# Fillings put between the two heads' transposes, rope taken sooner, and another order of query tiles in the last pair of heads

## The chip, the cores and the metric

One core of a Trainium2 chip runs the whole kernel. The metric is the device time of one execution in microseconds, lower being better.

## The reference

A decoder trunk of two layers over 1024 positions of width 1024, in float32. The change lies in layer 0, whose mixer feeds two head groups from one projection: eight heads A (dilated sliding-window softmax attention, head width 64, partial rotary) and four heads B (gated linear attention, GLA). Shortened:

```python
z = h @ w_in
qa, ka, va, qb, kb, vb, rb, gl = jnp.split(z, offs, axis=-1)
qa = partial_rope(split_heads(qa, N_HEADS_A), positions)
ka = partial_rope(split_heads(ka, N_HEADS_A), positions)
oa = dilated_attention(qa, ka, split_heads(va, N_HEADS_A))      # causal softmax, three dilations
ob = gla(split_heads(qb, N_HEADS_B), split_heads(kb, N_HEADS_B), split_heads(vb, N_HEADS_B), ...)
ob = rms_norm(ob, g_out_b) * jax.nn.silu(split_heads(rb, N_HEADS_B))
o = jnp.concatenate([merge_heads(oa), merge_heads(ob)], axis=-1)
return o @ w_out
```

A gated feed-forward layer follows, then layer 1 with its own feed-forward, and a last norm.

## The kernel before

Every float32 matrix product is made of three products of high and low parts (`hi*hi`, `lo*hi`, `hi*lo`). The eight heads A are worked in four pairs of heads (`hp` 0 to 3), the queries in tiles of 128 (`qt` 0 to 7). The loop of the attention goes over 32 *pairs* `n` of (pair of heads, query tile), in the order of `TILE_ORDER`. Since attention is causal, tile `qt` has `qt + 1` key tiles; they are handled in groups of four, so tiles 0 to 3 have one group (`groups(n) == 1`) and tiles 4 to 7 two. A *step* is one group of one pair. The queues of the engines are written out by hand, and each engine runs its queue in order.

TensorE (L1087 scores, L1100 transposes, L1108 and L1120 reciprocals and products with V) does at the first step of pair `n`: the *score block* of pair `n + 1` for both heads; a filling; the transposes of the first head's exponentials; the products of the step before; the transposes of the second head. Both heads' transposes use the same PSUM bank, so each waits until ScalarE has copied the one before (`take`, L2216). A *filling* is a number of pieces of the projections of the next pair of heads: 48 pieces of three 512-column matmuls each (L1019 to L1021) and two blocks of four transposes of V (T0 and T1, L1028), numbered 0 to 49. They end the parts V0 V1 T0 T1 K0 Q0 K1 Q1 with numbers 7, 15, 16, 17, 25, 33, 41 and 49, where 0 and 1 are the first and second half of the positions. `PIECES` says how many go into each filling. In the last pair of heads the fillings are pieces of the output projection instead (`wo_piece`, L1062 to L1064, by `WO_PIECES`). They need the split outputs of the heads, which ScalarE (`split_high`, L2220) and VectorE (`split_low`, L1694) make in the order of `WO_HIGHS` and `WO_LOWS`.

VectorE takes the row maximum of each head's score block (`top(U)`, L1660, `U = 2n + h`; the next score block waits for the maxima of the last pair), the reciprocals of the sums (`recip`, L1667 and L1671), the output (`take_out`, L1678 and L1680) and the projected parts: V by `take_v` (L1619), K and Q by `rope` in three stages (shuffle and two multiplications; sum and high part; low part: L1635 to L1648). In the first three pairs it also finishes the GLA heads (`out_step`, L1558 to L1571, 128x1024 each). ScalarE makes the exponentials (`exp`, L2205) and copies T0 and T1 (`take_vn`, L2196). GpSimd splits each weight in a high part (L594) and a low part (L597), once the projection that used the buffer has ended. Query tiles 4 to 7 need the rope of K1 and Q1:

```python
pe.wait_ge(A.rope, 20 * hp + (10 if qt < 4 else 20))
if n:
    pe.wait_ge(A.max, 2 * n)
```

## Time and profile before

| | |
|---|---|
| Time, median of 3 runs | 2145.39 us (2144.12 to 2146.19) |
| The profiled execution: its time, its span | 2148.89 us, 2147.1 us |
| TensorE busy | 2103.5 us (98%) |
| VectorE, ScalarE, GpSimd busy | 1486.9 us (69%), 877.8 us (41%), 882.1 us (41%) |
| Granted TensorE clock, mean | 0.996 |
| The attention's loop | from about 243 to 507 us of the span |

Busy time is the time in which an engine had an instruction running. Because TensorE is busy nearly throughout, time shows as lost where its rows carry an idle time in brackets, with what released it, or where a matmul takes longer than its like. Times in the timeline count from the start of the span.

### The profile page before, as it was taken

The page shows a single profiled execution, that of the slowest core. Times are in us where ns is not written, and L with a number is a line of the kernel's source. Part 1 is how long each engine was busy: PE and PEld are TensorE (multiplying, and loading weights), DVE is VectorE, ACT ScalarE, POOL GpSimd, SP SyncE. Part 2 cuts the span into 40 slices and gives each one's busy share as a digit, 9 for nine tenths or more (in the row PEclk, how much of TensorE's full clock was granted, in tenths as well). Part 3 has the DMA queues.
Part 4 walks back from the last instruction along what each step waited for, and adds up shares of the span by engine and source line. Part 5 has one row for each costly group of instructions (what it writes and reads, how often), then busy time and mean ns, then how long its engine had stood idle before and what let it go on. Part 6 is the DMA issues. An engine that isn't in the chain of part 4 may idle for free.

```text
span 2147.1 us, 26169 instructions
## 1 busy us (share of the span) xinstructions
PE 2103.5 (98%) x10190; PEld 1710.9 (80%) x10190; DVE 1486.9 (69%) x1663; ACT 877.8 (41%) x1122; POOL 882.1 (41%) x459
## 2 busy tenths in 40 slices
PE   8999899999999999999999999999999999999997
PEld 5878677767788888888888888888788888888886
DVE  6659865573796767767798803337967767686987
ACT  4231234352554444445344431025544444444444
POOL 4323211122387776772000333433776777730000
PEclk9999999999999999999999999999999999999999
DMA  4111000003322222214986111113222222239872
GB/s 167 40 30 40 30 21 21 21 21 118 118 82 86 89 89 85 82 70 159 389 297 252 59 40 40 43 46 128 79 88 79 81 76 89 89 107 378 311 282 79
DMA packets 95100, 236.10 MB, mean 110 GB/s; under 512 B 10082, under 2 KB 12419, under 8 KB 94979
## 3 DMA queue, kind: packets, MB, share of 16 engines
q1 hardware_dynamic: 93106, 229.70, 30.0%
q10 hardware_dynamic: 1872, 4.74, 0.6%
q8 instruction: 81, 1.33, 0.3%
q14 instruction: 41, 0.33, 0.0%
HBM read 198.75 MB, written 35.65 MB: 109 GB/s over the span
## 4 chain that ended last, share of the span: by engine, by line
PE 85%; DVE 9%; ACT 2%; issue 2%; DMA 2%; SPq 0%; DVEq 0%; ACTq 0%
PE ps L1214 12%; PE ps L1216 11%; PE ps L1215 11%; PE ps L1248 6%; PE ps L1250 6%; PE ps L1251 6%; PE ps L809 5%; PE ps L812 5%; PE ps L815 5%; PE ps L1019 2%; PE ps L1021 2%; PE ps L1020 2%; DMA d_ring<-g_kept 2%; PE ps L1100 1%; PE ps L1120 1%
## 5 line engine op out<-in xcount | busy, mean ns | idle before, releaser
L594 POOL TENSOR_TENSOR w_hi<-w_raw,ones 128x1024 fp32r<-128x1024 f32 x56 | 112.6, 2011 | 776.4 <-PE ps L815 235.6
L1214 PE MATMUL ps<-t_hi,w_hi 128*128 128x512 f32 x672 | 263.9, 393 | 1.9 <-ACT snap L2323 1.5
L1216 PE MATMUL ps<-t_hi,w_lo 128*128 128x512 f32 x672 | 261.7, 389 | 0.0
L1215 PE MATMUL ps<-t_lo,w_hi 128*128 128x512 f32 x672 | 261.6, 389 | 0.0
L1248 PE MATMUL ps<-d_hi 128*128 128x512 f32 (+1 forms) x640 | 244.7, 382 | 0.9 <-DVE d_lo L1910 0.7
L1251 PE MATMUL ps<-d_hi,d_lo 128*128 128x512 f32 (+1 forms) x640 | 243.9, 381 | 0.0
L1250 PE MATMUL ps<-d_lo,d_hi 128*128 128x512 f32 (+1 forms) x640 | 243.9, 381 | 0.0
L640 POOL TENSOR_TENSOR w_lo<-w_sum,w_hi 128x1024 fp32r<-128x1024 f32 x84 | 232.7, 2780 | 23.9 <-ACT w_hi L2326 23.9
L640 POOL TENSOR_TENSOR w_lo<-w_raw,w_hi 128x1024 fp32r<-128x1024 f32 x84 | 158.4, 1885 | 175.3 <-ACT w_hi L2326 157.5
L1214 PE MATMUL ps<-act_hi,w_hi 128*128 128x512 f32 x504 | 196.2, 389 | 0.7 <-POOL w_lo L640 0.7
L1215 PE MATMUL ps<-act_lo,w_hi 128*128 128x512 f32 x504 | 196.1, 389 | 0.0
L1216 PE MATMUL ps<-act_hi,w_lo 128*128 128x512 f32 x504 | 196.1, 389 | 0.0
L809 PE MATMUL ps<-act_hi,w_hi 128*128 128x512 f32 x592 | 185.2, 394 | 2.7 <-DVE act_lo L1408 1.3
L812 PE MATMUL ps<-act_lo,w_hi 128*128 128x512 f32 x592 | 182.5, 389 | 0.0
L815 PE MATMUL ps<-act_hi,w_lo 128*128 128x512 f32 x592 | 182.3, 389 | 0.0
L1214 PEld LDWEIGHTS ps<-t_hi,w_hi 128*128 128x128 f32 x672 | 126.1, 188 | 36.1 <-ACT snap L2323 10.3
L597 POOL TENSOR_TENSOR w_lo<-w_raw,w_hi 128x1024 fp32r<-128x1024 f32 x56 | 149.7, 2673 | 4.4
L2326 ACT ACTIVATE w_hi<-w_sum 128x1024 fp32r<-128x1024 f32 x84 | 89.1, 1061 | 151.5 <-PE ps L1216 111.0
L2310 ACT ACTIVATE ps<-fz,cw 128x1024 f32<-128x1024 f32 x88 | 105.6, 1202 | 108.1 <-DVE fz L1875 100.9
L1216 PEld LDWEIGHTS ps<-t_hi,w_lo 128*128 128x128 f32 x672 | 126.1, 188 | 26.5
L1215 PEld LDWEIGHTS ps<-t_lo,w_hi 128*128 128x128 f32 x672 | 126.2, 188 | 25.6
L1867 DVE TENSOR_TENSOR fz<-ps,snap 128x512 f32<-128x512 f32 x40 | 27.7, 692 | 167.2 <-PE ps L1216 167.2
(307 smaller groups left out, 4530.7 us busy)
## 6 DMA issues: line engine op xcount, KB each, us to landing
w_raw<-w_up SPq DMA_DIRECT2D x44, 1024.0 KB, 4.9
d_ring<-w_dn SPq DMA_DIRECT2D x146, 256.0 KB, 7.8
d_ring<-g_kept SPq DMA_DIRECT2D x124, 256.0 KB, 9.3
g_kept<-gst SPq DMA_DIRECT2D x44, 512.0 KB, 2.6
w_raw<-w_in SPq DMA_DIRECT2D x24, 512.0 KB, 3.6
chain_a<-g_kept SPq DMA_DIRECT2D x44, 256.0 KB, 8.9
x_kept<-x SPq DMA_DIRECT2D x16, 512.0 KB, 8.6
x<-x_kept SPq DMA_DIRECT2D x16, 512.0 KB, 10.2
```

What stands on the lines that cost most here:

```text
L594: pool.tensor_tensor(w_hi[:, slot, :], w_raw[:, parity, :], ones[:, 0:1].to_broadcast([P, 1024]), ALU.mult).then_inc(s_whi, 1)
L597: pool.tensor_tensor(w_lo[:, slot, :], w_raw[:, parity, :], w_hi[:, slot, :].bitcast(F32), ALU.subtract).then_inc(s_wsplit, 1)
L640: pool.tensor_tensor(w_lo[:, slot, cols].rearrange("p (a j c) -> p a j c", j=4, c=P), src, w_hi[:, slot, cols].bitcast(F32).rearrange("p ( ...
L809: pe.matmul(out[:, cols], wh, act_hi_k[:, cols], start=first, stop=False)
L812: pe.matmul(out[:, cols], wh, act_lo_k[:, cols], start=False, stop=False)
L815: ins = pe.matmul(out[:, cols], wl, act_hi_k[:, cols], start=False, stop=last)
L1214: pe.matmul(out, wh, bh, start=(fresh and j == 0), stop=False, skip_group_check=True)
L1215: pe.matmul(out, wh, bl, start=False, stop=False, skip_group_check=True)
L1216: ins = pe.matmul(out, wl, bh, start=False, stop=(j == 3), skip_group_check=True)
L1248: pe.matmul(out, w[:, 0, wcols], w[:, 1, cols], start=(s == 0 and i not in (D6, D7)), stop=False, skip_group_check=True)
L1250: pe.matmul(out, w[:, 0, wcols], g[:, 1, cols], start=False, stop=False, skip_group_check=True)
L1251: return pe.matmul(out, g[:, 0, wcols], w[:, 1, cols], start=False, stop=(s == NBLK - 1), skip_group_check=True)
```

## The change

TensorE's filling moves from ahead of a step's transposes to between them, and at pairs of two groups the second filling follows the first step's second transposes. ScalarE makes the next pair's exponentials ahead of the second head's copy. VectorE's order changes: the output of the pair before comes ahead of the reciprocals, the first two stages of a part's rope are taken together as soon as its pieces have ended, and some GLA steps come behind the parts. In the last pair of heads the order of query tiles changes from 1 2 3 0 4 5 6 7 to 3 2 7 6 5 4 1 0; the projections now end in its first pair (pair 24) instead of its second, and the pieces of the output projection and the splits of its operand are dealt out anew.

```diff
-        TILE_ORDER = (tuple(range(ST)),) * (NHP - 1) + ((1, 2, 3, 0, 4, 5, 6, 7),)
+        TILE_ORDER = (tuple(range(ST)),) * (NHP - 1) + ((3, 2, 7, 6, 5, 4, 1, 0),)
...
         PIECES = ((10,), (7,), (9,), (6,), (3, 3), (2, 2), (2, 2), (2, 2))
-        PIECES = (PIECES,) * 2 + (((8,), (8,), (7,), (5,), (2, 2), (2, 2), (2, 2), (2, 2)),
-                                  ((4,), (2,), (), (), (), (), (), ()))
+        PIECES = (PIECES,) * 2 + (((10,), (7,), (9,), (5,), (3, 2), (2, 2), (2, 1), (2, 1)),
+                                  ((4,), (), (), (), (), (), (), ()))
-        WO_HIGHS = ((), (0,), (1, 2), (3, 4), (5, 6), (), (), ())
+        WO_HIGHS = ((0,), (1, 2), (3, 4), (5,), (6,), (), (), ())
...
-                fill(n, gi)
                 transposes(n, gi, 0)
                 if step:
                     values(*steps[step - 1])
+                if gi == 0:
+                    fill(n, 0)
                 transposes(n, gi, 1)
+                if gi == 0 and groups(n) == 2:
+                    fill(n, 1)
...
+            B_STEPS = (((1, 0), (1, 1), (1, 2)), ((0, 0), (0, 1)), ((0, 3), (0, 4)))
+            B_LATE_STEPS = (((1, 3), (1, 4)), ((0, 2),), ())
             for n in range(PAIRS):
                 first_parts, second_parts = parts_of(n, 0), parts_of(n, 1) if groups(n) == 2 else []
                 if n + 1 < PAIRS:
                     top(2 * n + 2)
                     if groups(n) == 1:
                         top(2 * n + 3)
+                if n:
+                    take_out(n - 1)
                 recip(n)
                 if n < 3:
-                    for h, step_n in (((1, 0), (1, 1), (1, 2), (1, 3), (1, 4)), ((0, 0), (0, 1), (0, 2)), ((0, 3), (0, 4)))[n]:
+                    for h, step_n in B_STEPS[n]:
                         out_step(1, h, step_n)
-                if n == 0:
-                    take_part(0, Q1, (1,))
-                if n:
+                if n and n != ST * (NHP - 1) + 1:
                     for target, part in parts_of(n - 1, groups(n - 1) - 1):
                         take_part(target, part, (2,))
                 for target, part in first_parts:
                     take_part(target, part, (0,))
+                    take_part(target, part, (1,))
+                    if n == ST * (NHP - 1):
+                        take_part(target, part, (2,))
                 if n == 0:
-                    take_part(0, Q1, (2,))
-                if n:
-                    take_out(n - 1)
-                if groups(n) == 2 and n + 1 < PAIRS:
-                    top(2 * n + 3)
-                for target, part in first_parts:
-                    take_part(target, part, (1,))
-                for target, part in second_parts:
-                    take_part(target, part, (0,))
-                    take_part(target, part, (1,))
+                    take_part(0, Q1, (1, 2))
                 if groups(n) == 2:
+                    if n + 1 < PAIRS:
+                        top(2 * n + 3)
                     for target, part in first_parts:
                         take_part(target, part, (2,))
+                    for target, part in second_parts:
+                        take_part(target, part, (0,))
+                        take_part(target, part, (1,))
+                if n < 3:
+                    for h, step_n in B_LATE_STEPS[n]:
+                        out_step(1, h, step_n)
...
             for n in range(PAIRS):
+                take(n, 0, 0)
+                if n + 1 < PAIRS:
+                    exp(2 * n + 2)
+                    if groups(n) == 1:
+                        exp(2 * n + 3)
                 for gi in range(groups(n)):
                     for target, part in parts_of(n, gi):
                         if part == T0 or part == T1:
                             take_vn(target, part - T0)
-                    for h in range(2):
-                        take(n, gi, h)
-                    if gi == 0 and n + 1 < PAIRS:
-                        exp(2 * n + 2)
-                if n + 1 < PAIRS:
-                    exp(2 * n + 3)
+                take(n, 0, 1)
+                if groups(n) == 2:
+                    take(n, 1, 0)
+                    take(n, 1, 1)
+                    if n + 1 < PAIRS:
+                        exp(2 * n + 3)
```

TensorE's queue at pair 5 (first pair of heads, query tile 5), from behind the score block of pair 6; `a_s` are the exponentials and `a_pt` their copied transposes. Before:

```order
L1019 MATMUL ps<-act_hi,w_hi 128x512
L1020 MATMUL ps<-act_lo,w_hi 128x512
L1021 MATMUL ps<-act_hi,w_lo 128x512
L1019 MATMUL ps<-act_hi,w_hi 128x512
L1020 MATMUL ps<-act_lo,w_hi 128x512
L1021 MATMUL ps<-act_hi,w_lo 128x512
L1100 MATMUL ps<-cst,a_s 128x128 x4
L1120 MATMUL ps<-a_pt,a_vn_131 64x128 x2
L1100 MATMUL ps<-cst,a_s 128x128 x4
```

The same place in the changed kernel:

```order
L1100 MATMUL ps<-cst,a_s 128x128 x4
L1120 MATMUL ps<-a_pt,a_vn_131 64x128 x2
L1019 MATMUL ps<-act_hi,w_hi 128x512
L1020 MATMUL ps<-act_lo,w_hi 128x512
L1021 MATMUL ps<-act_hi,w_lo 128x512
L1019 MATMUL ps<-act_hi,w_hi 128x512
L1020 MATMUL ps<-act_lo,w_hi 128x512
L1021 MATMUL ps<-act_hi,w_lo 128x512
L1100 MATMUL ps<-cst,a_s 128x128 x4
```

The two pieces moved from ahead of the first head's four transposes to between these and the second head's.

VectorE's queue where the rope of K1 for the last pair of heads stands, which is pair 23 before (query tile 7) and pair 22 in the changed kernel (tile 6); L1660 and L1663 are row maxima, `a_sh` the rope's scratch. Before:

```order
L1635 STREAM_SHUFFLE a_sh_143<-ps 128x512
L1636 TENSOR_TENSOR a_sh_143<-ps,ropeC 128x512
L1638 TENSOR_TENSOR a_sh_143<-a_sh_143,ropeS 128x512
L1678 COPY a_r<-ps 128x128
L1680 TENSOR_TENSOR oT<-ps,a_r 128x128
L1660 ISA a_s,tiny<-ps,lmul 128x256
L1660 ISA tiny 128x1
L1643 TENSOR_TENSOR a_sh_143<-a_sh_143 128x512
L1645 CAST a_kh_134<-a_sh_143 128x512
L1648 TENSOR_TENSOR a_kl_137<-a_sh_143,a_kh_134 128x512
```

In the changed kernel, whose lines on VectorE are numbered 3 higher:

```order
L1638 STREAM_SHUFFLE a_sh_143<-ps 128x512
L1639 TENSOR_TENSOR a_sh_143<-ps,ropeC 128x512
L1641 TENSOR_TENSOR a_sh_143<-a_sh_143,ropeS 128x512
L1646 TENSOR_TENSOR a_sh_143<-a_sh_143 128x512
L1648 CAST a_kh_134<-a_sh_143 128x512
L1663 ISA a_s,tiny<-ps,lmul 128x1024
L1663 ISA tiny 128x1
L1651 TENSOR_TENSOR a_kl_137<-a_sh_143,a_kh_134 128x512
```

The row maximum of the second head, now of 1024 keys, moved behind the rope's sum and high part.

TensorE's queue from just behind the last piece of Q1 to the first score block of the last pair of heads that needs all keys (512 columns, then more). Before, this is from pair 25 on:

```order
L1100 MATMUL ps<-cst,a_s 128x128 x3
L1108 MATMUL ps<-cst,a_rows 128x128
L1120 MATMUL ps<-a_pt,a_vn_132 64x128 x4
L1100 MATMUL ps<-cst,a_s 128x128 x3
L1087 MATMUL ps<-a_kh_134,a_qh_136 128x128 x2
L1087 MATMUL ps<-a_kl_137,a_qh_136 128x128 x2
L1087 MATMUL ps<-a_kh_134,a_ql_141 128x128 x2
L1100 MATMUL ps<-cst,a_s 128x128 x4
L1108 MATMUL ps<-cst,a_rows 128x128
L1120 MATMUL ps<-a_pt,a_vn_132 64x128 x6
L1100 MATMUL ps<-cst,a_s 128x128 x4
L1087 MATMUL ps<-a_kh_134,a_qh_136 128x512 x2
```

In the changed kernel, with the last piece itself as its first three rows:

```order
L1019 MATMUL ps<-act_hi,w_hi 128x512
L1020 MATMUL ps<-act_lo,w_hi 128x512
L1021 MATMUL ps<-act_hi,w_lo 128x512
L1100 MATMUL ps<-cst,a_s 128x128 x4
L1087 MATMUL ps<-a_kh_134,a_qh_136 128x512 x2
L1087 MATMUL ps<-a_kl_137,a_qh_136 128x512 x2
L1087 MATMUL ps<-a_kh_134,a_ql_141 128x512 x2
```

Of what stood between the last piece and that score block, four transposes are left.

## Rows read from the trace of the kernel before

**Rows 1.** Busy time in stretches: one per pair of heads, then around 266.

```profile
core 0: us, PE busy (x) PEld busy (x) DVE busy (x) ACT busy (x) POOL busy (x), PEclk, DMA share, GB/s
242.80:315.80 73.00, 65.48 (x432) 50.58 (x432) 53.77 (x105) 24.53 (x59) 15.33 (x8) 0.95 0.08 26
315.80:381.40 65.60, 64.08 (x449) 49.58 (x448) 38.52 (x95) 24.84 (x58) 13.20 (x7) 1.00 0.08 25
381.40:442.50 61.10, 60.16 (x433) 46.22 (x432) 36.94 (x89) 24.92 (x58) 11.60 (x5) 1.00 0.06 19
442.50:506.70 64.20, 57.99 (x421) 43.31 (x421) 36.75 (x81) 31.20 (x63) 15.52 (x7) 1.00 0.25 89
...
262.60:269.40 6.80, 4.68 (x13) 3.89 (x14) 6.46 (x13) 0.60 (x1) 0.00 (x0) 0.52 0.25 77
```

**Rows 2.** What TensorE waited for: us in total, times, longest.

```profile
PE ps L1028 <- DVE a_vt L1619: 5.5, 1, 5.5
PE ps L1100 <- ACT a_pt L2216: 5.5, 15, 0.8
```

**Rows 3.** Timeline of TensorE: start, us, engine, line, [idle before, releaser].

```profile
264.72 1.12 PE L1028 MATMUL ps<-cst,a_vt 128*128 128x128 f32 x4 [5.53 <-DVE a_vt L1619]
```

**Rows 4.** Timeline of VectorE ahead of the end of that wait.

```profile
256.61 2.92 DVE L1558 SCALAR_TENSOR_TENSOR b_st<-b_st,b_kd 128x1024 f32<-128x1024 f32 x1
259.56 3.25 DVE L1562 TENSOR_TENSOR b_st<-b_st,b_kd 128x1024 f32<-128x1024 f32 x1
...
263.98 0.68 DVE L1619 TENSOR_TENSOR a_vt<-ps,rstd 128x512 f32<-128x512 f32 x1
```

**Rows 5.** Timeline of GpSimd at the same place and near 437.

```profile
256.48 1.96 POOL L594 TENSOR_TENSOR w_hi<-w_raw,ones 128x1024 fp32r<-128x1024 f32 x1 [9.66 <-PE ps L1021]
258.52 3.20 POOL L597 TENSOR_TENSOR w_lo<-w_raw,w_hi 128x1024 fp32r<-128x1024 f32 x1
...
437.33 1.89 POOL L594 TENSOR_TENSOR w_hi<-w_raw,ones 128x1024 fp32r<-128x1024 f32 x1 [37.37 <-PE ps L1021]
439.31 2.71 POOL L597 TENSOR_TENSOR w_lo<-w_raw,w_hi 128x1024 fp32r<-128x1024 f32 x1
```

**Rows 6.** Timeline of TensorE: transposes at pairs 0 and 5.

```profile
250.35 0.27 PE L1100 MATMUL ps<-cst,a_s 128*128 128x128 f32 x1
251.07 0.30 PE L1100 MATMUL ps<-cst,a_s 128*128 128x128 f32 x1 [0.46 <-ACT a_pt L2216]
...
294.21 0.60 PE L1100 MATMUL ps<-cst,a_s 128*128 128x128 f32 x4
...
295.58 0.63 PE L1100 MATMUL ps<-cst,a_s 128*128 128x128 f32 x4 [0.41 <-ACT a_pt L2216]
...
297.43 0.38 PE L1100 MATMUL ps<-cst,a_s 128*128 128x128 f32 x2
```

**Rows 7.** Timeline of ScalarE at pair 6.

```profile
305.04 1.15 ACT L2205 ACTIVATE a_s<-a_s,tiny 128x1024 f32<-128x1024 f32 x1
...
306.19 0.47 ACT L2216 ACTIVATE a_pt<-ps 128x384 f32<-128x384 f32 x1
```

**Rows 8.** Timeline of VectorE: the rope of K1 beside GpSimd.

```profile
437.23 0.74 DVE L1635 STREAM_SHUFFLE a_sh<-ps 128x512 f32<-128x512 f32 x1
...
438.45 1.32 DVE L1638 TENSOR_TENSOR a_sh<-a_sh,ropeS 128x512 f32<-128x512 f32 x1
...
440.56 2.00 DVE L1643 TENSOR_TENSOR a_sh<-a_sh 128x512 f32<-128x512 f32 x1
442.59 0.43 DVE L1645 CAST a_kh<-a_sh 128x512 fp32r<-128x512 f32 x1
```

**Rows 9.** Timeline of VectorE: first and last rows of an undisturbed rope.

```profile
211.56 0.73 DVE L1635 STREAM_SHUFFLE a_sh<-ps 128x512 f32<-128x512 f32 x1
...
214.85 0.69 DVE L1648 TENSOR_TENSOR a_kl<-a_sh,a_kh 128x512 fp32r<-128x512 f32 x1
```

**Rows 10.** Timeline of TensorE: pair 24's score block, the closing matmuls.

```profile
442.50 0.44 PE L1087 MATMUL ps<-a_kh,a_qh 64*128 64x384 f32 x2
...
495.67 0.50 PE L1062 MATMUL ps<-act_hi,w_hi 128*128 128x512 f32 x1
```

More of the change, by code:

```diff
@@ L770, in build @@
         PIECES = ((10,), (7,), (9,), (6,), (3, 3), (2, 2), (2, 2), (2, 2))
-        PIECES = (PIECES,) * 2 + (((8,), (8,), (7,), (5,), (2, 2), (2, 2), (2, 2), (2, 2)),
-                                  ((4,), (2,), (), (), (), (), (), ()))
-        WO_HIGHS = ((), (0,), (1, 2), (3, 4), (5, 6), (), (), ())
-        WO_LOWS = ((), (), (0, 1), (2, 3), (4, 5), (6,), (), ())
-        WO_PIECES = ((0,), (0,), (0,), (4,), (2, 2), (2, 1), (1, 1), (1, 0))
+        PIECES = (PIECES,) * 2 + (((10,), (7,), (9,), (5,), (3, 2), (2, 2), (2, 1), (2, 1)),
+                                  ((4,), (), (), (), (), (), (), ()))
+        WO_HIGHS = ((0,), (1, 2), (3, 4), (5,), (6,), (), (), ())
+        WO_LOWS = ((), (0, 1), (2, 3), (4,), (5,), (6,), (), ())
+        WO_PIECES = ((0,), (0,), (2, 2), (2, 2), (1, 1), (1, 1), (2,), (0,))
         def fill_of(n, gi):
```

## The prediction

> **What bounds the kernel.** I read the share of busy time first: TensorE is busy 98% of the span, so only its idle time and its slow clock can be won back. The table by stretches says where those are inside the attention [rows 1]: 7.5 us idle in the first pair of heads, 1.5 and 0.9 us in the second and third, 6.2 us in the last (length less busy time of each of the first four rows). The list of who waited for whom names the first: one wait of 5.5 us for `a_vt`, and 15 short ones for `a_pt`, 5.5 us together [rows 2]. It ends at 264.72 [rows 3]. From 262.6 to 269.4 the granted clock was at 0.52, the lower of its two levels (1.2 GHz), with 4.68 us of TensorE's work in it (the fifth of [rows 1]): half of that, 2.3 us, is what the slow clock costs on top.
>
> Why the wait was so long is in VectorE's queue: two operations on two SBUF tensors, 1.2 us each when alone, take 2.92 and 3.25 [rows 4], while GpSimd splits a weight [rows 5]. They alternate: GpSimd's first split ends at 258.44 and VectorE's operation 1.1 us behind it; the second split, 2.4 us when alone, takes 3.20, and VectorE's next one ends 1.1 us behind that.
>
> **The change, part by part.** Times are relative to the trace of before; every instruction stays, so only waits and the overlap count.
>
> *Filling between the transposes (small waits).* At a step with one key group the second head's transposes start 0.72 us after the first's, where alone they need 0.11; with four key tiles 1.37 where work allows 0.96 [rows 6]. With a filling between, this is gone: -0.6 at pair 0, -0.36 at pairs 1 and 9, -0.4 at pairs 5, 13 and 21. In return a pair's first transposes now follow the last pair's second ones with only one score block between. The same 1.37 us holds there; where that block is short (the head changes at pairs 8 and 16, the pairs before them) it gives 1.14 and 0.96: +0.2 each, four times.
>
> *The 5.5 us wait.* TensorE stood there from 259.2 (264.72 less 5.53). It now comes 1.0 us sooner by pairs 0 and 1, but has pair 2's first transposes and pair 1's products (1.2 us) ahead: about 259.5. VectorE takes V's second half behind two GLA steps instead of three, but those two wait for GpSimd as before. Its queue by its own durations: the reciprocals' copy is held to 258.7, then a split of 2.4 us and two steps of 1.2 us: 263.4, against 263.98 [rows 4]. So the transposes start at 264.15, 0.6 sooner, and 1.2 us of work is already done: with pair 0's 0.6, which lies inside that wait and isn't added again, -1.75 in all. The wait is still about 4.6 us, and I take the clock to fall as before.
>
> *ACT's new order.* `exp` of the next pair's first head now stands ahead of this pair's second copy of the transposes, `take`. At pair 6 that `exp` starts at 305.04, because its row maxima stand behind K1's rope steps, and the next copy only at 306.19 [rows 7]. Count from the second group's transposes of pair 5, 297.43 [rows 6]: this copy then starts at +8.8 and pair 6's second group can be transposed at +9.5; by its own work TensorE is there at +7.9, so 1.6 us are lost. Before, 0.2 and 0.7 were lost there and some slack used: the stretch to the next score block was 10.92 us and becomes 11.54, +0.6 at pairs 6 and 14. Sum so far, first two pairs of heads: -1.75 - 0.4 + 0.6 + 0.4 = -1.15 and -0.36 - 0.4 + 0.6 + 0.4 = +0.25.
>
> *Third pair of heads.* Its pieces now end K1 at pair 22's first filling and Q0's first half at pair 20's. All of that rope's first two stages stand ahead of the second row maximum, on which the next score block waits. Pair 20: rope ends 3.1 us behind the filling, the maximum 0.95 later, TensorE is ready at 3.45: +0.85. Pair 22: K1's end also sets GpSimd going. The row shows what that does: from the shuffle at 437.23 the steps that take 0.68 alone took 1.32 and 2.00, and the cast began 5.36 us behind the shuffle [rows 8]. In before a score maximum and an output stood between and nobody waited. Now the maximum of 1024 keys (1.15 us) comes behind the cast: it ends 7.1 us behind the filling, while TensorE, after four transposes (0.4), a piece (0.8), three transposes (0.3), the products (1.2) and three transposes (0.5), is ready at 3.2: a wait of +3.9. Won: -0.1, -0.5 (pairs 17, 18: the two blocks of V transposes are apart), -0.4, -0.25. Sum: +0.85 + 3.9 - 1.25 = +3.5.
>
> The Trainium skill ("SBUF — State Buffer", section "SBUF: two separate sides") calls the port that VectorE and GpSimd share an exclusive lock, held by whichever started first for the whole instruction; the trace agrees, 2.00 us against 0.68. If they only slowed each other a little, the wait at pair 22 would be 1.3 us by the undisturbed rows.
>
> *Last pair of heads.* Query tile 7 comes third. Its scores need all of K and Q, and Q's last piece ends only in the filling just ahead. A rope that nothing disturbs takes 3.98 us from shuffle to the last low part [rows 9]; with 0.2 to start, TensorE, which has four transposes (0.59), waits 3.5 us at that score block. From there I went along the queues with the durations of before: waits of 0.5 and 0.4 us for the 1024-key maxima and exponentials, 0.4 at tile 6, 0.6 at tiles 5 and 4, 0.5 at the last two; then the 48 closing matmuls start 50.1 us behind the first score block, and two pieces (1.36 us) less are in it than in the 53.17 us of before [rows 10]. 51.46 against 53.17: -1.7. Its bounds: each `act_lo` operand or `take` one queue place later costs about 1 us, so -4 to +3.
>
> *The clock.* Before fell to half behind 5.5 us of idling. Two new waits idle TensorE 3.7 and 3.3 us. No row shows a wait between 2 and 5 us and what the clock did. Bounds: nothing, or the 2.3 us above each. They are nearer to the known wait than to none: I take 1.8 and 1.2 (the second partly hides under the next wait for VectorE).
>
> Sum: -1.15 + 0.25 + 3.5 - 1.7 = +0.9; with the clock +3.0: **+3.9 us**. It is made against the profiled execution (span 2147.1 us, 2148.9 with what lies around it), which is 3.5 above the median of the three runs; the difference carries over: 2145.4 + 3.9 = **2149.3 us**. 0.2% is 4.3 us, about what a measurement of this kernel can tell from no change, so this is within it, near its edge.
>
> **Rivals.**
> *A, the sum above*, 2149.3, own range 2145 to 2153.5 (a microsecond or so in each of the four stretches): 0.48.
> *B, the clock stays up at the new waits.* They are shorter than the one that is known to drop it. 2146.3; if it also stays up at the first, now 4.6 us: 2144.0. 0.2.
> *C, slower: in the last pair of heads copies queue behind exponentials.* Four large tiles follow each other; VectorE has `split_low` (1.2 us) and ScalarE `split_high` (1 us) ahead of each first maximum and copy. My walk gives 0.4 per tile because the short fillings just cover it. Once a first maximum ends over a microsecond later than I have it, each of the four pays pair 6's 1.6 us: 4 x 1.2 more, 2154.1. For it: [rows 7]. Against: the walk has slack at two of them. 0.2.
> *D, faster: VectorE gets ahead of GpSimd.* If its operations ask for the port first where the new order shifts them by tenths, the first wait shrinks to 0.9 us (-3.7) and the clock stays up (-2.3), pair 22 waits 1.3 instead of 3.9 (-2.6) with no fall (-1.8), and pairs 6 and 14 don't wait (-3.2): 2135.7. Against it: in every case of [rows 4, 8] VectorE was the one held. 0.12.
>
> **How the numbers follow.** Beyond 2149.7 lies somewhat under half of A and nearly all of C: slower 0.38. Faster (below 2141.1): most of D, and an error of mine in A or B: 0.18. Within: 0.44. The range, 2139 to 2155.5, holds A, B, most of C and a third of D.
>
> **What would show it.** In the profile after: a wait of 4 to 5 us at the transposes of V's second half, near 260; one near 3.9 us at the score block behind pair 22, released by a row maximum; one near 3.5 us at the first score block of 1024 keys of the last heads, released by `a_ql`; the waits of the first transposes for `a_pt` below 0.3 us, with 1.6 us at pairs 6 and 14. Wrong would make me: neither new wait over 2 us; a score block that another row releases; the last pair of heads shorter than 48 us or longer than 53 from its first score block of 384 keys to the 48 closing matmuls.

## The result, and the profile after

The changed kernel takes 2150.8 us (median of 9 runs, 2150.05 to 2155.05), the kernel before beside it 2145.6 us (9 runs, 2144.12 to 2148.29). The ratio is 1.0023, with a 95% interval from 1.0014 to 1.0031. That is 4.9 us slower by the ratio and 5.2 by the two medians, where +3.9 was forecast; 2150.8 stands against a forecast of 2149.3.

The profiled execution took 2151.1 us. Its page, the span and the first row of busy time:

```profile
span 2149.3 us, 26169 instructions
...
PE 2106.8 (98%) x10190; PEld 1713.0 (80%) x10190; DVE 1490.2 (69%) x1663; ACT 879.0 (41%) x1122; POOL 883.9 (41%) x459
```

The share is 98% as before, so the page says nothing more. The stretches say where the time went. This is the answer to the same question as [rows 1], cut at the score blocks that are issued in pairs 0, 8, 16 and 24 and at the closing matmuls; the last three lines are the stretches at half clock:

```profile
core 0: us, PE busy (x) PEld busy (x) DVE busy (x) ACT busy (x) POOL busy (x), PEclk, DMA share, GB/s
240.25:311.96 71.71, 65.94 (x432) 50.78 (x432) 53.16 (x105) 24.71 (x59) 15.36 (x8) 0.95 0.09 26
311.96:377.84 65.88, 64.10 (x449) 49.51 (x448) 38.89 (x95) 25.03 (x58) 13.15 (x7) 1.00 0.08 25
377.84:446.38 68.54, 63.50 (x439) 48.34 (x438) 38.59 (x91) 25.77 (x58) 11.52 (x5) 0.98 0.08 24
446.38:498.93 52.55, 47.71 (x367) 34.91 (x366) 31.65 (x74) 29.95 (x62) 12.00 (x6) 0.94 0.06 19
260.37:267.20 6.83, 6.08 (x17) 4.93 (x18) 6.25 (x13) 2.00 (x5) 0.00 (x0) 0.50 0.25 76
437.87:441.28 3.41, 3.41 (x23) 2.10 (x19) 0.73 (x3) 2.00 (x5) 0.00 (x0) 0.50 0.03 12
454.93:461.76 6.83, 5.84 (x33) 4.16 (x33) 3.18 (x6) 2.04 (x4) 0.00 (x0) 0.50 0.00 0
```

With before cut in the same way, its score blocks at 242.82, 315.80, 381.42 and 442.50 and the closing matmuls at 495.67 [rows 10], the four parts are:

| us in the part | 1st pair of heads | 2nd | 3rd | last | loop |
|---|---|---|---|---|---|
| before | 72.98 | 65.62 | 61.08 | 53.17 | 252.85 |
| after | 71.71 | 65.88 | 68.54 | 52.55 | 258.68 |

The loop is 5.8 us longer. The spans differ by 2.2 only (2149.3 against 2147.1), because this execution was 2.6 us sooner at its first score block and 1.1 shorter behind the loop, where the profile of before has a stretch at half clock (at 1242) that this one hasn't. The medians, 5.2 apart, side with the loop. So I read causes from parts of the loop, and gains from medians and ratios.

Who waited for whom, TensorE's rows of the loop (us in total, times, longest). The first line holds the row maxima that score blocks waited for (3.75, 0.91, and one of 1.03 at the loop's start, 1.05 before). [Rows 2] are the answer of before to the two lines behind it, and the last line is new:

```profile
engine line waited for: us in total, times, longest us
PE ps L1087 <- DVE tiny L1663: 5.7, 3, 3.8
PE ps L1100 <- ACT a_pt L2223: 4.1, 7, 1.4
PE ps L1028 <- DVE a_vt L1622: 4.1, 1, 4.1
PE ps L1087 <- DVE a_ql L1651: 3.6, 1, 3.6
```

And these waits one by one, in the timeline of TensorE:

```profile
261.12 1.12 PE L1028 MATMUL ps<-cst,a_vt 128*128 128x128 f32 x4 [4.10 <-DVE a_vt L1622]
...
302.22 0.52 PE L1100 MATMUL ps<-cst,a_s 128*128 128x128 f32 x3 [1.37 <-ACT a_pt L2223]
...
418.39 0.50 PE L1087 MATMUL ps<-a_kh,a_qh 64*128 64x512 f32 x2 [0.91 <-DVE tiny L1663]
...
437.44 0.50 PE L1087 MATMUL ps<-a_kh,a_qh 64*128 64x512 f32 x2 [3.75 <-DVE tiny L1663]
...
455.92 0.80 PE L1087 MATMUL ps<-a_kh,a_qh 64*128 64x512 f32 x2 [3.64 <-DVE a_ql L1651]
```

The wait of pair 6 stands a second time at 368.10, pair 14, with the same 1.37. The other waits for `a_pt` are 0.19 to 0.23, and one of 0.56 at 495.50. Each of the five waits shown is one that the prediction named, with its releaser: 4.6 forecast for the first (4.10 seen), 1.6 (1.37), 0.85 (0.91), 3.9 (3.75) and 3.5 (3.64).

Behind the two at 302 and 437 stand these rows of ScalarE, VectorE and GpSimd:

```profile
300.36 1.15 ACT L2212 ACTIVATE a_s<-a_s,tiny 128x1024 f32<-128x1024 f32 x1 [2.90 <-DVE tiny L1663]
...
301.50 0.57 ACT L2223 ACTIVATE a_pt<-ps 128x512 f32<-128x512 f32 x1
...
431.62 1.32 DVE L1641 TENSOR_TENSOR a_sh<-a_sh,ropeS 128x512 f32<-128x512 f32 x1
433.04 2.65 DVE L1646 TENSOR_TENSOR a_sh<-a_sh 128x512 f32<-128x512 f32 x1
435.73 0.43 DVE L1648 CAST a_kh<-a_sh 128x512 fp32r<-128x512 f32 x1
436.07 1.22 DVE L1663 CUSTOM_DVE_ANT_0 a_s<-ps,lmul 128x1024 f32<-128x1024 f32 x1
...
430.50 1.89 POOL L594 TENSOR_TENSOR w_hi<-w_raw,ones 128x1024 fp32r<-128x1024 f32 x1 [32.99 <-PE ps L1021]
432.47 2.68 POOL L597 TENSOR_TENSOR w_lo<-w_raw,w_hi 128x1024 fp32r<-128x1024 f32 x1
```

The copy at 301.50 that pair 6's transposes wait for had been ready to go and stood behind an exponential that itself had waited 2.90 us for its row maximum. At 433 the rope's sum ends 0.5 us behind GpSimd's split, and the row maximum that the score block needs stands behind both. Of the new waits, two are followed by a slow clock: 3.4 us of it from 437.9, 6.8 us from 454.9.

### The profile page after: what moved, and what is told of

The parts are those of the page before. It is cut to its first block, busy times and chain, and to the rows that moved or that the text cites. A ratio compares the mean times of both kernels' runs of the same rounds, so it can differ in the third digit from the quotient of the medians.

```text
span 2149.3 us, 26169 instructions
## 1 busy us (share of the span) xinstructions
PE 2106.8 (98%) x10190; PEld 1713.0 (80%) x10190; DVE 1490.2 (69%) x1663; ACT 879.0 (41%) x1122; POOL 883.9 (41%) x459
## 3 DMA queue, kind: packets, MB, share of 16 engines
q8 instruction: 81, 1.33, 0.3%
## 4 chain that ended last, share of the span: by engine, by line
PE 88%; DVE 8%; issue 2%; ACT 1%; DMA 0%; SPq 0%; DVEq 0%; ACTq 0%
PE ps L1217 12%; PE ps L1218 12%; PE ps L1219 11%; PE ps L1251 7%; PE ps L1253 6%; PE ps L1254 6%; PE ps L809 5%; PE ps L812 5%; PE ps L815 5%; PE ps L1019 2%; PE ps L1021 2%; PE ps L1020 2%; PE ps L1100 2%; PE ps L1120 2%; PE ps L1322 1%
```

## The experiments

In all of them the kernel before ran beside. They stand in the order of running. Parts of the loop are given at the end, in one table; each comes from one execution.

**e1_rope_later.** Where a pair has two key groups, the rope's sum and high part go behind the second row maximum:

```diff
                     take_part(target, part, (0,))
-                    take_part(target, part, (1,))
+                    if groups(n) == 1:
+                        take_part(target, part, (1,))
...
                     for target, part in first_parts:
-                        take_part(target, part, (2,))
+                        take_part(target, part, (1, 2))
```

> At pairs of two key groups VectorE takes the rope's sum and high part behind the second row maximum again, everything else as changed. My account (the row maximum stood behind a rope held up by GpSimd): the wait of 3.75 us at the score block behind pair 22 falls to about 0.8, the 0.9 us at pair 20 goes, and the clock doesn't fall there (2.1 us): about -6, 2144.8 us. Rival (the wait is GpSimd's or ScalarE's, and the maximum only the last in a row of late things): the wait stays above 2 us, released by another row, and the time stays within 2 us of 2150.8.

2144.57 us, ratio to before 0.9991 (0.9982 to 1.0000). Its timeline, TensorE's score block and VectorE's rows:

```profile
432.07 0.49 PE L1087 MATMUL ps<-a_kh,a_qh 64*128 64x512 f32 x2 [0.53 <-DVE tiny L1663]
...
430.70 1.21 DVE L1663 CUSTOM_DVE_ANT_0 a_s<-ps,lmul 128x1024 f32<-128x1024 f32 x1
431.84 1.72 DVE L1646 TENSOR_TENSOR a_sh<-a_sh 128x512 f32<-128x512 f32 x1
```

The maximum goes ahead of the held operation; the wait is 0.53 instead of 3.75, the 0.91 of pair 20 is gone, and the clock stays up here. The third part of the loop is 5.7 shorter (62.83 against 68.54), about all of the 5.8 that the change lost. The first and last parts are 1.5 and 0.6 shorter too, but that is no work of the edit: their waits of 4.1 and 3.6 us are still there, and the slow clock behind each lasts 3.4 us in this execution instead of 6.8.

**e2_gla_later.** The two GLA steps ahead of V's second half go behind it:

```diff
-            B_STEPS = (((1, 0), (1, 1), (1, 2)), ((0, 0), (0, 1)), ((0, 3), (0, 4)))
-            B_LATE_STEPS = (((1, 3), (1, 4)), ((0, 2),), ())
+            B_STEPS = (((1, 0), (1, 1), (1, 2)), (), ((0, 3), (0, 4)))
+            B_LATE_STEPS = (((1, 3), (1, 4)), ((0, 0), (0, 1), (0, 2)), ())
```

> The two GLA steps that stand ahead of V's second half at pair 1 come behind it, everything else as changed. My account: the wait of 4.1 us at the transposes of V's second half goes to below 0.3 us, and with it the fall of the clock (2.9 us): about -7, 2143.9 us. Rival (the steps only move, and the maxima of pair 3 come late instead): a wait of 3 us or more appears at a score block or at exponentials of pairs 2 to 4, and the time falls by less than 3 us.

2146.05 us, 0.9997 (0.9988 to 1.0007). Its timeline, VectorE and then the longest wait that is left to TensorE near this place (the 1.36 of pair 6 is still there):

```profile
255.12 1.54 DVE L1674 COPY a_rows<-tiny 128x128 f32<-128x128 f32 x1
256.58 0.68 DVE L1622 TENSOR_TENSOR a_vt<-ps,rstd 128x512 f32<-128x512 f32 x1
257.18 2.93 DVE L1561 SCALAR_TENSOR_TENSOR b_st<-b_st,b_kd 128x1024 f32<-128x1024 f32 x1
...
265.80 0.63 PE L1100 MATMUL ps<-cst,a_s 128*128 128x128 f32 x4 [0.56 <-ACT a_pt L2223]
```

The 4.10 us are gone and the slow clock with them, and no wait of 3 us came at pairs 2 to 4. The first part is 6.3 us shorter (65.40 against 71.71), where about 7 were expected; the median is 4.8 lower, 2.2 short of the expectation. The held step still takes 2.93 us, now with nobody behind it: the loss came from who stood in line behind a held operation.

**e3_split_later.** GpSimd's next split waits for the row maxima of the third pair of heads, so that it is out of the rope's way, and nothing in VectorE's queue moves:

```diff
-            plain(N_WO, 0, (s_proj, R_WO - 1))
+            plain(N_WO, 0, (s_proj, R_WO - 1), (A.max, 16 * (NHP - 1)))
```

> GpSimd splits the first weight of the output projection only behind the last row maximum of pair 23, everything else as changed: VectorE's order is untouched. If the port that VectorE and GpSimd share makes the rope late, its sum takes 0.7 us instead of 2.65, the wait behind pair 22 falls from 3.75 to about 1.2 us and the clock stays up: about -4.6, 2146.2 us. Rival (the rope and the maximum by themselves are what is late): the wait stays above 3 us and the time stays.

2146.0 us, 1.0000 (0.9991 to 1.0009). Its timeline, VectorE, TensorE, GpSimd:

```profile
430.88 0.68 DVE L1641 TENSOR_TENSOR a_sh<-a_sh,ropeS 128x512 f32<-128x512 f32 x1
431.66 0.69 DVE L1646 TENSOR_TENSOR a_sh<-a_sh 128x512 f32<-128x512 f32 x1
...
434.10 0.50 PE L1087 MATMUL ps<-a_kh,a_qh 64*128 64x512 f32 x2 [1.15 <-DVE tiny L1663]
...
434.13 2.19 POOL L594 TENSOR_TENSOR w_hi<-w_raw,ones 128x1024 fp32r<-128x1024 f32 x1 [37.35 <-DVE tiny L1663]
```

The same two operations take 0.68 and 0.69 us here, against 1.32 and 2.65 beside GpSimd. So of the 3.75 us, 2.6 are GpSimd's and 1.15 the rope's own length. The later output projection weight costs nothing.

**e4_tile_order.** Tile 1 comes third in the last pair of heads (3, 2, 1, 7, 6, 5, 4, 0), so that its work covers the rope; the output projection's places follow:

```diff
-... + ((3, 2, 7, 6, 5, 4, 1, 0),)
+... + ((3, 2, 1, 7, 6, 5, 4, 0),)
-        WO_HIGHS = ((0,), (1, 2), (3, 4), (5,), (6,), (), (), ())
-        WO_LOWS = ((), (0, 1), (2, 3), (4,), (5,), (6,), (), ())
+        WO_HIGHS = ((0,), (1, 2), (3,), (4,), (5,), (6,), (), ())
+        WO_LOWS = ((), (0, 1), (2,), (3, 4), (5,), (6,), (), ())
-        WO_PIECES = ((0,), (0,), (2, 2), (2, 2), (1, 1), (1, 1), (2,), (0,))
+        WO_PIECES = ((0,), (0,), (2,), (2, 2), (2, 2), (1, 1), (1, 1), (0,))
```

> Query tile 1 comes third in the last pair of heads (3 2 1 7 6 5 4 0), so that one more pair stands between Q's last piece and the first score block of 1024 keys; the output projection's pieces are dealt out to fit. My account: the wait of 3.64 us for the rope of Q falls to about 1.1 us and the clock doesn't fall there (2.2 us): about -4.7, 2146.1 us, give or take 1.5 for the pieces that moved. Rival (the four large tiles then stand later, and their copies and exponentials stall the short fillings): the saved time comes back as waits for a_pt or act_lo behind it, less than 2 us in all.

2151.66 us, 1.0029 (1.0017 to 1.0040). My expectation of 2146.1 failed by 5.6 us; the rival's held. Its timeline of TensorE, from the slowest of its seven executions (2155.78):

```profile
459.05 0.50 PE L1087 MATMUL ps<-a_kh,a_qh 64*128 64x512 f32 x2 [1.51 <-DVE tiny L1663]
...
464.69 0.50 PE L1087 MATMUL ps<-a_kh,a_qh 64*128 64x512 f32 x2 [0.90 <-DVE tiny L1663]
...
486.11 0.50 PE L1062 MATMUL ps<-act_hi,w_hi 128*128 128x512 f32 x1 [1.84 <-DVE act_lo L1697]
...
493.78 0.50 PE L1062 MATMUL ps<-act_hi,w_hi 128*128 128x512 f32 x1 [1.71 <-DVE act_lo L1697]
```

The wait for `a_ql` is gone, and four others, 6.0 us together, are there in its place: two for row maxima, which the rival hadn't named, and two for `act_lo`, which it had. Covering a late result by moving a tile moved every operand of the output projection too.

**e5_old_tables.** The new queues with all the tables of before (`TILE_ORDER`, `PIECES`, `WO_HIGHS`, `WO_LOWS`, `WO_PIECES`: the `-` lines of the change's diff), and without the early low part in pair 24.

> The new queues (fillings between the transposes, the exponential ahead of the second copy) with the tile order, the pieces and the output projection's places of before. My theory: the two stalls of the third pair of heads come from the pieces' new ends and go: the score block behind pair 22 waits under 0.3 us, that of pair 20 too. But before ended K1's first half at pair 23's filling and Q0's at pair 21's, and now only one block of transposes and a score block follow such a filling before the row maximum is needed. So the same stall should come one pair later, at the score block behind pair 23, 2 to 4 us, with the fall of the clock, and 0.5 to 1 us behind pair 21. The 3.64 us wait for a_ql in the last heads is gone with its slow clock (2.2). Expected: 2150.8 - 3.6 (a_ql and clock) + 1.5 (its last heads as long as in before, less the clock), about 2148.5. Rival: the stall belongs to the new tables alone and the queues are a gain by themselves: no wait over 1 us from pair 17 to the end, 2142.5 or less. A third: the queues are what costs, at pairs with four key groups, and it stays at 2151.

2148.86 us, 1.0013 (1.0004 to 1.0022), as expected. The stall comes one pair later and shorter; its timeline, VectorE, then TensorE:

```profile
438.36 2.66 DVE L1646 TENSOR_TENSOR a_sh<-a_sh 128x512 f32<-128x512 f32 x1
...
441.96 0.44 PE L1087 MATMUL ps<-a_kh,a_qh 64*128 64x384 f32 x2 [2.31 <-DVE tiny L1663]
```

So the stall belongs to the queues, which put every such rope ahead of a row maximum, and the tables only set its size. The wait for `a_ql` I had thought to be the new tables' alone. It is there, with 2.01 us: the rope's high part ends at 454.17, and its low part starts at 455.37 only, behind two row maxima and an output. And 1.79 us for a copy came at 478.

**e6_act_order.** At pairs with two key groups, ACT copies the second head's transposes ahead of the next pair's exponential:

```diff
                 take(n, 0, 0)
+                if groups(n) == 2:
+                    take(n, 0, 1)
                 if n + 1 < PAIRS:
                     exp(2 * n + 2)
...
-                take(n, 0, 1)
+                if groups(n) == 1:
+                    take(n, 0, 1)
```

> At pairs with two key groups ACT takes the second head's copy of the first group ahead of the next pair's exponential, as before; where one group is all, nothing changes. My theory: the three-times 1.37 us waits for a_pt behind the exponential at pairs 6 and 14 are that order's price; what is left of each is 0 to 0.2, and the exponential 0.57 later delays nothing by more than 0.1. Expected 2148.1 (2150.8 - 2 x 1.37). Rival: the wait is only moved, since the exponential stands behind K1's rope anyway and the next pair's first copy comes just as late; then 2150.8 stays.

2148.4 us, 1.0011 (1.0002 to 1.0020). Both waits of 1.37 are gone, and nothing stands in their place: the second part is 1.33 shorter. The first is 2.86 shorter, of which some 1.7 are again a slow stretch that lasts 3.4 us here instead of 6.8. The stalls at 414 to 452 stay (0.89, 3.74, 3.64).

**e7_q_sooner.** The third pair of heads gives its pieces out as the first two do, which ends Q of the last heads in pair 23:

```diff
-        PIECES = (PIECES,) * 2 + (((10,), (7,), (9,), (5,), (3, 2), (2, 2), (2, 1), (2, 1)),
-                                  ((4,), (), (), (), (), (), (), ()))
+        PIECES = (PIECES,) * 3 + (((),) * ST,)
```

> The third pair of heads gives its projection out as the first two do, so that Q and K of the last heads end by pair 21 and their own last pieces stand in no filling of the last pair of heads. The clocks' falls behind the 3.75 us and 3.64 us waits are what I want to see go with them. My theory: won are 0.9 (pair 20), 3.75 with the slow clock's 2.0 (pair 22), 3.6 with its 2.2 (a_ql); given back are what two-group pairs of the second heads show, 1.4 at pair 22, and 0.4 at the head change, and up to 1.5 of the absorbed waits at the next maxima. Sum about -9: 2142. Rival: the time goes into other waits in the last heads, because without two pieces there the fillings are shorter and VectorE, not the late Q, sets the pace: 2147 or more.

2141.41 us, 0.9977 (0.9968 to 0.9986), below before by more than its interval. The 0.91 and 3.75 of the third pair of heads are gone, the wait for `a_ql` is 1.07, and the clock falls only behind the first wait. Given back are 1.43 us for a copy at pair 22, by the same order of ACT's queue as at pairs 6 and 14.

**e8_together.** The edits of e7_q_sooner, e1_rope_later, e2_gla_later and e6_act_order in one kernel.

> The edits of the last one, of e1_rope_later, e2_gla_later and e6_act_order in one kernel. If the stalls are separate, each gives what it gave alone: 2142 as expected of the pieces given out sooner, -4.7 (the first wait and its slow clock), -2.7 to -4 (ACT's order at pairs 6, 14 and 22), the later rope nothing more, since its stall is gone already: 2134. If the stalls share slack, so that taking one away lengthens the next one, it stays above 2139.

2130.92 us, 0.9933 (0.9920 to 0.9947): 10.5 us faster than e7_q_sooner alone. Of the loop's 10.0 the first part gives 7.1, the second 1.2, the third 1.3, the last 0.4. I had expected 2134; what was too small there was the first wait, put at 4.7 with its slow clock. By parts, each edit gives here about what it gave alone, so the stalls were separate. No stretch at half clock is left in the loop.

**e9_tables_alone.** The kernel before with the new tables; its old queues stay, but for Q's low part in pair 24, which that score block needs and which would else stand behind its row maximum:

```diff
-                if n:
+                if n and n != ST * (NHP - 1) + 1:
...
                 for target, part in first_parts:
                     take_part(target, part, (1,))
+                    if n == ST * (NHP - 1):
+                        take_part(target, part, (2,))
```

> The kernel before with the four new tables (tile order, pieces, the projection's places) and all of Q's last rope in pair 24, but with the old order of TensorE's, VectorE's and ACT's queues. My theory: the 3.75 us wait is the product of a table (K1's first half ends at pair 22's filling) and a queue (the rope ahead of the next row maximum), so it isn't here: no wait over 1 us for a row maximum at the score block behind pair 22 or 23. The wait for a_ql is the tables' alone and comes here too, about 3 us, since in the old order the products of pair 23 stand between the filling and that score block. Third pair of heads +1.4 (two pieces more), last one 52.5 against 53.2 with its slow clock: 2146.9, no difference to before. Rival: the tables cost by themselves what the change lost, 2150.8; another: without the stall at pair 24 and with a_ql hidden they are a gain, 2144 or less.

2146.8 us, 1.0005 (0.9996 to 1.0014). Its timeline, VectorE at pair 22, then TensorE:

```profile
432.68 1.23 DVE L1660 CUSTOM_DVE_ANT_0 a_s<-ps,lmul 128x1024 f32<-128x1024 f32 x1 [0.16 <-PE ps L1100]
...
433.82 0.94 DVE L1643 TENSOR_TENSOR a_sh<-a_sh 128x512 f32<-128x512 f32 x1
...
450.00 0.50 PE L1087 MATMUL ps<-a_kh,a_qh 64*128 64x512 f32 x2 [2.36 <-DVE a_ql L1648]
```

K1's rope stands in pair 22 here too, next to the same split on GpSimd, and costs TensorE nothing, since the maximum is ahead of the sum. The wait for `a_ql` is 2.36, where 3 was expected. The new tables alone are no loss.

**e10_old_queues.** Before, with the tables of e7_q_sooner: the price of the queues with the stalls away.

> The kernel before with the tables of e7_q_sooner: new tile order, Q and K of the last heads projected by pair 23, old queues. Against e7_q_sooner this prices the queues alone, with the stalls of the third pair of heads gone in both. My theory: the new queues give 1.3 in the first pair of heads, nothing in the second and third, and 1 to 1.5 in the last, where four large tiles follow each other. Expected 2144.2. Rival: the queues are worth nothing without stalls, 2142.5 or less; or they are what makes the late wait short, and it stays at 2146 or more.

2143.26 us, 0.9985 (0.9976 to 0.9994). Against e7_q_sooner its parts are 1.6 longer, 0.2 shorter, the same and 0.6 shorter. The new queues win in the first pair of heads alone, where their later GLA step counts; in the last, where I had looked for a gain of 1 to 1.5, they lose 0.6 (here there is no wait for `a_ql`, in e7_q_sooner one of 1.07). The two intervals overlap.

**e11_low_sooner.** e8_together, with the low part of Q's last rope ahead of the maxima of pair 24:

```diff
-                if n and n != ST * (NHP - 1) + 1:
+                if n and n != ST * (NHP - 1):
...
-                    if n == ST * (NHP - 1):
-                        take_part(target, part, (2,))
...
                         take_part(target, part, (1,))
+                        if n == ST * (NHP - 1) - 1:
+                            take_part(target, part, (2,))
```

> e8_together with the low part of Q's last rope taken in pair 23 itself, ahead of the row maxima of pair 24. My theory: the wait of 1.06 us for a_ql at the first score block of 1024 keys goes, and the row maxima of pair 24 come 0.7 later, which costs up to 0.3 at that score block: 2130.2, not to be told from 2130.9 by the times, but in the profile's waits. Rival: the wait only changes its name to a row maximum, with the same length, and nothing is won.

2129.34 us, 0.9924 (0.9910 to 0.9938), the lowest median of all; its interval and that of e8_together overlap. Its stretches:

```profile
239.78:303.90 64.12, 63.25 (x433) 48.86 (x433) 52.68 (x105) 24.40 (x59) 14.39 (x8) 1.00 0.09 29
303.90:368.43 64.53, 64.13 (x451) 49.63 (x450) 38.71 (x95) 24.94 (x58) 13.17 (x7) 1.00 0.08 25
368.43:433.28 64.85, 64.50 (x450) 49.72 (x449) 39.46 (x96) 25.32 (x58) 11.21 (x5) 1.00 0.08 26
433.28:477.06 43.78, 42.08 (x356) 31.12 (x355) 29.49 (x70) 29.83 (x62) 12.02 (x6) 1.00 0.08 24
```

TensorE idles 3.3 us in 237.3 (length less busy time of the four rows), and the clock is at full in each. The wait of 1.06 for `a_ql` is gone and the next maximum's is 0.43, against 0.47 in e8_together; the last part is 1.2 shorter.

**e12_old_tile_order.** e8_together with the old tile order and the old places of the output projection.

> e8_together with the old order of the last heads' query tiles (1 2 3 0 4 5 6 7) and the old places of the output projection. It prices the tile order where no stall is in the way. My theory, from the last pair of heads in e5_old_tables less its pieces, its wait for a_ql and its slow clock: 48.2 us against 44.95, because the two largest tiles end the chain and nothing stands between their exponentials and products: 2134.2. Rival: the order is worth nothing once the stalls are gone, 2131.

2132.59 us, 0.9938 (0.9924 to 0.9951). The last part, in its stretch, against 44.95 in e8_together:

```profile
433.13:479.40 46.27, 42.50 (x356) 31.02 (x355) 30.77 (x70) 29.94 (x62) 14.44 (x6) 1.00 0.11 35
```

The new order is worth 1.3 us in the profile, less than half of the 3.2 expected: I had taken e5_old_tables' last part as the order's own, and the 1.79 us for a copy that are in it aren't here. The two intervals overlap, so the times alone don't tell.

The parts of the loop of all kernels, cut as above:

| | 1st | 2nd | 3rd | last | loop | median us |
|---|---|---|---|---|---|---|
| before | 72.98 | 65.62 | 61.08 | 53.17 | 252.85 | 2145.6 |
| after | 71.71 | 65.88 | 68.54 | 52.55 | 258.68 | 2150.8 |
| e1_rope_later | 70.25 | 65.83 | 62.83 | 52.00 | 250.91 | 2144.6 |
| e2_gla_later | 65.40 | 65.85 | 68.55 | 52.56 | 252.36 | 2146.1 |
| e3_split_later | 71.11 | 65.85 | 64.43 | 52.56 | 253.95 | 2146.0 |
| e4_tile_order | 71.70 | 65.85 | 68.53 | 53.61 | 259.69 | 2151.7 |
| e5_old_tables | 71.50 | 65.83 | 64.48 | 55.96 | 257.77 | 2148.9 |
| e6_act_order | 68.85 | 64.55 | 68.59 | 51.58 | 253.57 | 2148.4 |
| e7_q_sooner | 71.21 | 65.82 | 66.09 | 45.39 | 248.51 | 2141.4 |
| e8_together | 64.11 | 64.59 | 64.84 | 44.95 | 238.49 | 2130.9 |
| e9_tables_alone | 72.68 | 65.60 | 63.38 | 51.32 | 252.98 | 2146.8 |
| e10_old_queues | 72.83 | 65.60 | 66.11 | 44.77 | 249.31 | 2143.3 |
| e11_low_sooner | 64.12 | 64.53 | 64.85 | 43.78 | 237.28 | 2129.3 |
| e12_old_tile_order | 64.10 | 64.60 | 64.58 | 46.27 | 239.55 | 2132.6 |

The third and the last column hold different numbers of pieces (0.68 us each) in different kernels: 46 and 4 in after, e1 to e4, e6 and e9, 44 and 6 in before and e5, 50 and none in e7, e8 and e10 to e12.

## Why the prediction was right, and where its terms were off

The mechanism and the places were right. The forecast sum was 0.9 without the clock and 3.9 with it; the loop shows about +1.4 and +5.8.

*First pair of heads.* Forecast -1.15, seen -1.27. Up to the score block of 270.36 it is -1.70 against -1.75. e2_gla_later shows the cause: it is the GLA steps ahead of V's second half that TensorE waits for, three in before and two in after. Pair 6 cost 1.37 where 1.6 was forecast; what follows the score block of 270.36 comes to +0.43 (forecast +0.6). e6_act_order shows that this was ACT's order, and that it could be had back. The near hit hides two errors. The wait fell to 4.10, not to 4.6, and the slow clock, taken to cost what it did, cost 0.5 more: TensorE was at work sooner, so 6.08 us of its work and no longer 5.00 fell into the slow stretch.

*Second pair.* +0.25 forecast, +0.26 seen.

*Third pair.* This is the first term that was mis-sized. The part is 7.46 longer. Of that, 1.36 are two pieces moved in from the last pair, and 1.5 the slow clock (from the score block at 437.44 to the next there are 8.94 us, in e1_rope_later, where the clock stays up, 7.44; half of the 3.41 us of work in the stretch would be 1.7). The 4.6 that are left stand against +3.5. The two waits are 0.91 and 3.75, as forecast; the net gain of 1.25 that I had around them isn't there. A term that I left out is 0.35 of it: the score block of pair 24, which this part ends with, is now that of tile 3 with 512 keys (0.90 us in e9_tables_alone) and no longer that of tile 1 (0.55).

*Last pair.* From its first score block 50.1 us were forecast. 52.55 are seen, 50.1 to 50.4 without the slow clock, so that the walk along the queues was right to 0.3 us: -1.4 to -1.7 against -1.7. That is in part luck. The wait of 3.64 is there, but behind it the walk had small waits of 0.5, 0.4, 0.4, 0.6 and 0.5; e1_rope_later, with less slow clock to hide them, shows 0.32, 0.16, 0.56 and 0.17. e4_tile_order failed where no such walk was made.

*The clock* is the second mis-sized term: 1.8 + 1.2 were forecast on top of before's, 1.5 + 2.4 and the 0.5 of the first pair of heads are seen. No row of before stood behind either number, so that one came near is luck. For the second I had counted on a slow stretch whose cost hides under the next wait for VectorE. It had 5.84 us of work in it, 2.9 us of cost, and only 0.5 was there to hide it: in e1_rope_later, where that stretch is 3.4 us, the next two waits are 0.32 and 0.16. The prediction also cut before's own stretch 0.3 us early (262.60 for 262.89), which gave it 4.68 us of work and 2.3 of cost in place of 5.00 and 2.5.

That a slow stretch costs half of TensorE's work in it is shown by the first pair of heads, whose queues are the same in five kernels. As they stand the parts differ by 0.6; less half of the work in the stretch they differ by 0.05:

| | first part | work in its slow stretch | part less half of that |
|---|---|---|---|
| after | 71.71 | 6.08 | 68.67 |
| e3_split_later | 71.11 | 4.83 | 68.69 |
| e4_tile_order | 71.70 | 6.05 | 68.67 |
| e5_old_tables | 71.50 | 5.61 | 68.69 |
| e7_q_sooner | 71.21 | 5.13 | 68.64 |

The three kernels with the old queues give 70.48 (before), 70.50 (e9_tables_alone) and 70.52 (e10_old_queues) in the same way. So the new queues won 1.8 us of waits there, and the clock took part of it back.

*The rivals.* B (clock stays up) fell at once. C (copies queue behind exponentials in the last heads) did not happen: no wait for `a_pt` over 0.6 us stands there in the profile after; its mechanism is what happened at pairs 6, 14, and in e5_old_tables, where the largest tiles end the chain. D (VectorE ahead of GpSimd) happened once, near 256, and won nothing of note:

```profile
255.97 1.21 DVE L1561 SCALAR_TENSOR_TENSOR b_st<-b_st,b_kd 128x1024 f32<-128x1024 f32 x1
257.21 3.25 DVE L1565 TENSOR_TENSOR b_st<-b_st,b_kd 128x1024 f32<-128x1024 f32 x1
...
256.04 3.33 POOL L597 TENSOR_TENSOR w_lo<-w_raw,w_hi 128x1024 fp32r<-128x1024 f32 x1
```

VectorE's first step starts 0.07 us ahead of GpSimd's split and takes its 1.21; the split takes 3.33 instead of 2.4, and VectorE's next step stands behind it. At pair 22 VectorE was the one held, and e3_split_later shows what D would have given there, 2.6 us of wait and the fall of the clock.

*The Trainium skill* ("SBUF — State Buffer", section "SBUF: two separate sides"), whose exclusive lock the prediction weighed against a slight slowing: e3_split_later settles it for this place. With GpSimd away the wait is 1.15; the slight slowing would have given 1.3 with GpSimd there, and 3.75 was seen. The same section limits the lock to operations on VectorE with two SBUF inputs or in a mode that uses both ports; here too the runs agree: the row maximum from PSUM takes 1.21 us beside the split in e1_rope_later and 1.22 in e3_split_later without it.

*What it comes to.* The tables alone are not to be told from no change (1.0005), the queues with the old tables are a little slower (1.0013), and both together 1.0023. Without the pieces that end Q in the last pair of heads, and with four placements mended, the same idea is 0.9924. Of the 21.4 us by which the loop of e11_low_sooner is shorter than after's, some 7 are slow clock (half of the 15.3 us of work in after's three slow stretches, less what was hidden), and the rest waits. That sum is worked out; no run took a wait away and left its slow stretch.

## What to carry to other kernels

Before an operation is put sooner in a queue, ask what was ahead of whom: here a rope's sum and high part placed ahead of the row maximum cost 5.7 us, and the same rope beside the same split on GpSimd cost nothing behind it. Place each operation by who waits for it, and price two engines that share a port by their held durations, not by those alone. And where a chain is walked from a trace of before, walk every operand of a table that moves with it: the one expectation made without that walk (e4_tile_order) was the one that failed by 5.6 us.

## What the runs showed of the hardware

Half clock follows waits much shorter than the 5.5 us that were known, but not all of them. The granted clock's slow stretches were 3.4 or 6.8 us long. Behind 4.10 us: 6.8 in after and in e3, e4, e5 and e7, 3.4 in e1_rope_later and e6_act_order. Behind 3.64: 6.8 in after, e2 and e3, 3.4 in e1_rope_later and e6_act_order. Behind 3.75: 3.4. Behind 2.36 (e9_tables_alone), 2.01 and 1.79 (both e5_old_tables) and 1.71 (e4_tile_order): 3.4. Behind 2.31 in e5_old_tables and behind 1.84 in e4_tile_order: nothing. Two stretches of e5_old_tables, behind the wait of 2.31 and behind that of 2.01:

```profile
441.96:445.30 3.34, 3.34 (x29) 2.58 (x30) 2.39 (x9) 2.07 (x7) 0.00 (x0) 1.00 0.33 131
457.75:461.16 3.41, 3.41 (x20) 2.79 (x21) 3.34 (x10) 1.92 (x5) 0.00 (x0) 0.50 0.01 2
```

TensorE is busy throughout both, and the granted clock is 1.00 in the first and 0.50 in the second. Nor is an idle TensorE needed. In before, far behind the loop, the clock is at half for 3.4 us where the profile shows no idle time for 20 us ahead of it, only sixteen matmuls of one column:

```profile
1239.44 1.94 PE L1340 MATMUL ps<-ones,rstd 1*128 1x1 f32 x16
...
1242.52:1245.93 3.41, 3.41 (x9) 2.68 (x9) 0.19 (x1) 3.35 (x9) 0.00 (x0) 0.50 0.00 0
```

The same stands there in e1, e4, e6, e9, e10 and e12; in after and the other six the same sixteen matmuls are followed by no fall. So the length of the wait alone doesn't decide it, and the same wait in two kernels can cost one stretch or two; what else decides stays open.

A held operation goes both ways between VectorE and GpSimd: VectorE's sum of 128x512 took 2.65 us behind a split and 0.69 without one (e3_split_later), and GpSimd's split took 3.33 us behind a step of VectorE and 2.4 without one.
